# PEER expert stage of a hybrid encoder block: 40 of 256 tokens by gathered rows, 216 densely, values in column form

## The reference, cut to what matters

```
q = x @ w_q                          # 8 heads x 2 halves x 128
s1, i1 = top16(q[h,0] . keys[h,0]);  s2, i2 = top16(q[h,1] . keys[h,1])
best, ci = top16(s1 + s2)            # 16 of 256 pairs per head
idx = e1*128 + e2;  g = softmax(best)    # 128 experts per token
act = gelu(x . u_tab[idx])
out = sum over the 128 picks of g * act * v_tab[idx]
```

## Time and profile before

| what | us |
|---|---|
| median of 3 runs (2036.15 to 2037.81) | 2036.79 |
| span of the profiled execution, first to last instruction | 2033.2 |
| PE busy (share of the span) | 1985.5 (98%) |
| DVE busy | 1344.0 (66%) |
| ACT busy | 864.8 (43%) |
| POOL busy | 318.4 (16%) |
| moved by DMA | 356.87 MB, mean 176 GB/s |

### The profile page before, as it was taken

The page is one execution under the profiler, slowest core; times in us unless marked ns, Lnnn a source line. Parts: engine busy times, 40 slices in busy tenths (PEclk is TensorE's granted clock), DMA queues, the critical chain, the costliest instruction groups (busy, mean ns, idle before and its releaser), DMA issues.

```text
span 2033.2 us, 32153 instructions
## 1 busy us (share of the span) xinstructions
PE 1985.5 (98%) x10414; PEld 1694.7 (83%) x10414; DVE 1344.0 (66%) x2052; ACT 864.8 (43%) x1085; POOL 318.4 (16%) x228
## 2 busy tenths in 40 slices
PE   8999979899999999999999999999999999999997
PEld 6887768788878888888888888888888888888886
DVE  4447765554898963466666666777777766666665
ACT  5544644444444444433333334333333334444444
POOL 1003320000434444311111111111111110000000
PEclk9999989999999999999999999999999999999999
DMA  7665435554555555554454455555555556666664
GB/s 250 186 186 152 143 114 183 200 194 158 186 173 188 174 188 186 186 165 160 161 163 160 161 165 179 183 165 165 166 164 164 164 158 218 195 192 191 194 193 148
DMA packets 97137, 356.87 MB, mean 176 GB/s; under 512 B 10864, under 2 KB 10896, under 8 KB 96320
## 3 DMA queue, kind: packets, MB, share of 16 engines
q1 hardware_dynamic: 95472, 347.65, 54.0%
q0 software_dynamic: 1184, 6.00, 0.9%
q10 hardware_dynamic: 432, 2.62, 0.4%
HBM read 352.03 MB, written 4.19 MB: 175 GB/s over the span
## 4 chain that ended last, share of the span: by engine, by line
PE 89%; DVE 6%; ACT 1%; DMA 1%; issue 1%; DVEq 0%; ACTq 0%; SPq 0%
PE PS L1071 24%; PE PS L1049 16%; PE PS L1054 15%; PE PS L1081 12%; PE PS L1058 8%; PE PS L1052 8%; PE PS L1231 5%; DVE LO L598 2%; DMA RAW<-wq_t 1%; PE PS L1024 1%; ACT HI L309 0%; PE PS L1260 0%; DVE store L799 0%; DVE CI L817 0%; DVE CAND L830 0%
## 5 line engine op out<-in xcount | busy, mean ns | idle before, releaser
L309 ACT ACTIVATE HI<-RAW 128x1024 fp32r<-128x1024 f32 x656 | 696.2, 1062 | 1035.2 <-DMA RAW<-peer_v 356.2
L598 DVE TENSOR_TENSOR LO<-RAW,HI 128x1024 fp32r<-128x1024 f32 x576 | 710.3, 1233 | 591.0 <-PE PS L1054 343.6
L1071 PE MATMUL PS<-xT,HI 128*128 128x512 f32 x2304 | 596.0, 396 | 2.0 <-DVE xT L625 1.2
L1071 PEld LDWEIGHTS PS<-xT,HI 128*128 128x128 f32 x2304 | 414.6, 189 | 74.7 <-issue 1.4
L1081 PEld LDWEIGHTS PS<-xT,LO 128*128 128x128 f32 x2304 | 313.7, 190 | 30.3 <-DVE LO L598 7.4
L1081 PE MATMUL PS<-xT,LO 128*128 128x256 f32 x2304 | 321.1, 282 | 6.1 <-DVE LO L598 6.1
L1049 PE MATMUL PS<-HI,WHL 128*128 128x512 f32 x1020 | 320.2, 395 | 1.3 <-DVE WHL L933 1.3
L1054 PE MATMUL PS<-HI,WHL 128*128 128x512 f32 x1020 | 314.7, 390 | 0.0
L1054 PEld LDWEIGHTS PS<-HI,WHL 128*128 128x128 f32 x1020 | 191.4, 188 | 40.4
L298 POOL TENSOR_TENSOR ONE<-ONE,EG 128x256 f32<-128x256 f32 x128 | 113.2, 884 | 706.6 <-DVE ONE L899 706.6
L1049 PEld LDWEIGHTS PS<-HI,WHL 128*128 128x128 f32 x1020 | 186.8, 188 | 36.6 <-DVE store L799 1.6
(11 more groups left out here) (168 smaller groups left out, 1249.5 us busy)
## 6 DMA issues: line engine op xcount, KB each, us to landing
RAW<-u_t SPq DMA_DIRECT2D x256, 512.0 KB, 3.7
RAW<-peer_v SPq DMA_DIRECT2D x256, 512.0 KB, 5.0
RAW<-w_in SPq DMA_DIRECT2D x80, 512.0 KB, 3.7
RAW<-w_out SPq DMA_DIRECT2D x32, 512.0 KB, 3.8
RAW<-wq_t SPq DMA_DIRECT2D x32, 512.0 KB, 4.7
x_spill<-X POOLq DMA_DIRECT2D x2, 1024.0 KB, 11.7
ACC<-x_spill ACTq DMA_DIRECT2D x2, 1024.0 KB, 9.4
out<-ACC SPq DMA_DIRECT2D x4, 512.0 KB, 3.7
```

The source lines that it names most:

```text
L309: nc.scalar.activation(HI[:, slot, :], RAW[:, slot, :], ACT.Copy).then_inc(hi_ready, 1)
L598: v.tensor_tensor(LO[:, u % 2, :], RAW[:, u % 4, :], HI[:, u % 4, :].bitcast(FP32), ALU.subtract).then_inc(lo_ready[u % 2], 1)
L1071: return mm(PS[:, bank, :], HI[:, u % 4, cols], xT[:, k].rearrange("p a t -> p (a t)"), start=k == 0, stop=k == KT - 1)
```

## The change

216 tokens (ND) stay dense. The last 40 (NS) are computed by gathered rows. For these, three picks of each token lie on 3 x 40 = 120 partitions (SROWS), so that the 128 picks need 43 steps (NG): POOL gathers 120 rows of u_tab (8 KB each) by an indirect DMA into PICKED; DVE multiplies by the token rows X4 and sums (`dot`); after 43 of these one gelu and one gate multiply; then 43 gathers of rows of v_tab, each added to ACC4 by DVE with its factor. There is one PICKED buffer, so each gather waits for the DVE instruction before it. Dots stand at 24 score steps three key indices apart (49 to 118), at 121, 123, 125, 127, and at value units 2 to 58, every fourth; additions at units 64 to 232, every fourth.

Score units: 8 matmuls of 432 and 8 of 216 columns; the low parts of unit n-1 are interleaved with the high parts of unit n. Value units take the column form too: the v_tab tile is stationary, WHL streams (432 and 216 columns), all 128 key indices accumulate in 8 PSUM banks for one half of the width, then for the other; no flushes by group, but a turn between the halves and a transposition at the end. The ring has 6 slots, LO overwrites RAW. One spread of 3 tokens covers all key indices: 72 in all, from key index 48 on. For key indices past 48 + b the gates are copied into `store` by ACT (`put_gates`) and the gelu result is multiplied in later (`land`). The tile with the 40 tokens is chosen first (TILE_ORDER). POOL also moves the token rows for X4 and reads the picks back through DRAM. The low parts that POOL makes: the odd units from 5 on in the score stage, every fourth in the value stage.

```diff
-TOKB = 4
-N_BATCH = T // TOKB
-E2A = NKEYS // 2
+NS, ND = 40, 216
+SLOTS, NG = 3, 43
+SROWS = SLOTS * NS
+TILE_ORDER = (1, 0)
+CHOICE0 = 2
+TOKB = 3
+N_BATCH = ND // TOKB
+SPREAD0 = 48
+SPREAD_END = SPREAD0 + N_BATCH
+DOT_STEPS = list(range(SPREAD0 + 1, SPREAD_END - 1, 3)) + list(range(SPREAD_END + 1, NKEYS, 2))
+DOT_UNITS = [2 + 4 * i for i in range(NG - len(DOT_STEPS))]
+ACC0 = DOT_UNITS[-1] + 6
+ACC_UNITS = [ACC0 + 4 * i for i in range(NG)]
+def by_pool(n):
+    return n % 2 == 1 and 5 <= n < N_U or n >= N_U and n % 4 == 3
...
+            def low(n):
+                pool.wait_ge(top_ready, n + 1)
+                nc.gpsimd.tensor_tensor(RING_LO[:, n % RING, :], RING_RAW[:, n % RING, :],
+                                        HI[:, n % HI_SLOTS, :].bitcast(FP32), ALU.subtract).then_inc(low_pool, 1)
+            def gather(table, g):
+                pool.indirect_dma_start(PICKED[0:SROWS, :], None, table,
+                                        bass.IndirectOffsetOnAxis(PK4[0:SROWS, 0, g:g + 1], 0)).then_inc(row_ready, 16)
...
+            for v in range(N_V):
+                if by_pool(N_U + v):
+                    low(N_U + v)
+                if v - 1 in DOT_UNITS:
+                    g = len(DOT_STEPS) + DOT_UNITS.index(v - 1) + 1
+                    pool.wait_ge(dots, g)
+                    if g < NG:
+                        gather(peer_u, g)
+                    else:
+                        gather(peer_v, 0)
+                if v - 1 in ACC_UNITS[:-1]:
+                    g = ACC_UNITS.index(v - 1) + 1
+                    pool.wait_ge(accs, g)
+                    gather(peer_v, g)
...
+            def top(n):
+                act.wait_ge(ring_ready[n % RING], 16 * (n // RING + 1))
...
+                    act.wait_ge(top_used, n - HI_SLOTS + 1)
+                    act.wait_ge(low_pool if by_pool(n - HI_SLOTS) else low_dve, LOW_COUNT[n - HI_SLOTS])
+                nc.scalar.activation(HI[:, n % HI_SLOTS, :], RING_RAW[:, n % RING, :], ACT.Copy).then_inc(top_ready, 1)
...
+            def dot(g):
+                dve.wait_ge(row_ready, 16 * (g + 1))
+                v.tensor_tensor_reduce(PICKED[0:SROWS, :], PICKED[0:SROWS, :], X4[0:SROWS, :], 1.0, 0.0, ALU.mult, ALU.add,
+                                       DOTS[0:SROWS, g:g + 1]).then_inc(dots, 1)
...
+            for j in range(NKEYS):
+                low(2 * j + 2)
+                low(2 * j + 3)
+                sum_halves(j)
+                if j >= CHOICE0:
+                    piece()
+                    piece()
+                b = j - SPREAD0
...
+                if 0 < b <= N_BATCH:
+                    apply_gates(b - 1)
+                if 0 <= b < N_BATCH:
+                    one_hots(b)
+                if b > 0:
+                    land(j - 1)
+                if j in DOT_STEPS:
...
+                    dot(DOT_STEPS.index(j))
+            land(NKEYS - 1)
...
+            for u in range(N_V):
+                low(N_U + u + 2)
+                if u + 2 < N_V:
+                    weight_lo(u + 2)
+                if u == NKEYS - 1:
+                    for i in range(DT):
+                        flush(0, i, OUTA)
+                if u in DOT_UNITS:
+                    dot(len(DOT_STEPS) + DOT_UNITS.index(u))
...
+                if u in ACC_UNITS:
+                    g = ACC_UNITS.index(u)
+                    dve.wait_ge(row_ready, 16 * (NG + g + 1))
+                    if g:
+                        dve.wait_ge(accs, g)
+                        ins = v.scalar_tensor_tensor(ACC4[0:SROWS, :], PICKED[0:SROWS, :], DOTS[0:SROWS, g:g + 1],
+                                                     ACC4[0:SROWS, :], ALU.mult, ALU.add)
...
+            for n in range(N_U):
+                j = n // 2
+                pe.wait_ge(top_ready, n + 1)
...
+                if n:
+                    low_wait(n - 1)
+                for kk in range(DT):
+                    ins = score_high(n, kk)
...
+                    if n:
+                        ins = score_low(n - 1, kk)
...
+                if n % 2 == 0 and 0 <= j - 2 - SPREAD0 < N_BATCH:
+                    spread(j - 2 - SPREAD0)
```

More of the change, by code:

```diff
@@ L305, in _ @@
+            pool.wait_ge(x1_back, 16 * TT)
+            pool.wait_ge(accs, NG)
+            for s in range(SLOTS):
+                if s:
+                    pool.wait_ge(sparse_added, 16 * s)
+                pool.dma_start(X1R[S0:P, TT - 1, :], ACC4[s * NS:(s + 1) * NS, :], accum_op=ALU.add)\
+                    .then_inc(sparse_added, 16)
         @block.scalar
@@ new lines, in _ @@
+            for n in range(4):
+                top(n)
+            for j in range(NKEYS):
+                top(2 * j + 4)
+                top(2 * j + 5)
+                if j in (2, 4):
+                    first_scores_out(j // 2 - 1)
+                if j in GATES_AT:
+                    gates_exp(GATES_AT.index(j))
+                if j in PICKS_AT:
+                    picks_to_rows(PICKS_AT.index(j))
+                if 0 <= j - 1 - SPREAD0 < N_BATCH:
+                    put_gates(j - 1 - SPREAD0)
+                gelu(j)
@@ new lines, in weight_hi @@
+            def weight_hi(v):
+                j = v % NKEYS
+                if v >= W_SLOTS:
+                    act.wait_ge(low_used, N_U + v - W_SLOTS + 1)
+                if v < NKEYS:
+                    act.wait_ge(g_mul, N_BATCH)
+                    if j >= SPREAD0:
+                        act.wait_ge(landed, j - SPREAD0 + 1)
+                nc.scalar.activation(WHL[:, v % W_SLOTS, 0, :], store[:, j, :], ACT.Copy).then_inc(w_hi, 1)
+            for v in range(3):
+                weight_hi(v)
@@ new lines, in _, with final_squares @@
+            for v in range(N_V):
+                if N_U + v + 4 < N_U + N_V:
+                    top(N_U + v + 4)
+                if v + 3 < N_V:
+                    weight_hi(v + 3)
+                if v == DOT_UNITS[-1] + 2:
+                    act.wait_ge(dots, NG)
+                    nc.scalar.activation(DOTS[0:SROWS, :], DOTS[0:SROWS, :], ACT.Gelu_apprx_tanh).then_inc(dots_gelu, 1)
+            nc.scalar.activation(GM[:, 2, 0:1], GM[:, 1, 0:1], ACT.Sqrt).then_inc(warm, 1)
+            def final_squares(tt, half):
+                act.wait_ge(out_added, (2, 4, 6, 8)[2 * half + tt])
+                if tt:
+                    act.wait_ge(sparse_added, 16 * SLOTS)
+                squares(X1R[:, tt, half * HALF:(half + 1) * HALF], 2 * half + tt, FJ[:])
@@ L980, in _, with piece @@
-            values(0, first=True)
-            values(1, second=True)
-            with dve.Fori(2, SPREAD2 - 1) as g:
-                values(g)
-            values(SPREAD2 - 1, next_late=True)
-            values(SPREAD2, spread=False, late=True)
-            with dve.Fori(SPREAD2 + 1, N_VG - 1) as g:
-                values(g, spread=False)
-            values(N_VG - 1, spread=False, next_late=True)
+            def piece():
+                o = 0 if done[0] < PIECES else 1
+                if done[o] < PIECES:
+                    next(pieces[o])
+                    done[o] += 1
@@ L1301, in _, with low_wait, score_high @@
-            values(0, first=True)
-            with pe.Fori(1, SPREAD2) as g:
-                values(g)
-            pe.wait_ge(g_read, 2 * N_BATCH)
-            with pe.Fori(SPREAD2, N_VG - 1) as g:
-                values(g, spreads=False)
-            values(N_VG - 1, spreads=False, last=True)
+            def low_wait(n):
+                pe.wait_ge(low_pool if by_pool(n) else low_dve, LOW_COUNT[n])
+            def score_high(n, kk):
+                j, half = divmod(n, 2)
+                k = DT * half + kk
+                return mm(PS[:, j % S_BANKS, 0:2 * ND].rearrange("p (a t) -> p a t", a=2),
+                          HI[:, n % HI_SLOTS, kk * P:(kk + 1) * P], xT[:, k, :, 0:ND], start=k == 0, stop=False)
```

660 lines of the change are left out of this document (339 added, 321 removed).

## The result

The change takes 2200.3 us (median of 4 runs, 2187.3 to 2209.7) where the kernel before takes 2037.3: a ratio of 1.079, 95% interval 1.074 to 1.084. It is 163 us slower, forecast was 87 us faster. The profiled execution took 2192.5 us, with a span of 2190.7.

The account below looks back on a forecast made before the run. PE, busy 98% of the span, was taken as the bound. Start 475.4, score stage 776, value stage 674 and end 21.6 gave 1947 us of span, plus 3.6 around it 1951, say 1950, against 2036.8; range 1850 to 2055.

Parts of the forecast that it names:

- ACT 1.4 us per unit. These fit.: Value stage: ACT's 1.4 us per unit and DVE's 7.5 of 9.45 us per four units fit beside PE's work.
- the landing of 8.0 us: Value stage: a gather lands 8.0 us after issue, 7.1 for size plus 0.9 for indices and ring; cycle 10.5 us.
- the dots of the score stage: Score stage: 24 dots beside spreads stall PE, 23 us at least, 80 with POOL's low part in front; 45 taken.
- ACT waiting on RING loads: A sign that would show the prediction wrong: ACT waits for the ring's loads; no size given.
- The matmul steps: Both stages: high steps 196.7 (scores) or 193.4 ns (values), lows 102.1; 1217 us for 256 units of each, against 1411.
- rival 1: Both stages: all hidden, gathers land within 7 us, DVE and POOL seldom collide; 1833 us, half way 1870; chance 0.25 together.
- rival 3: Value stage: the gather chain becomes the bound, each us of landing costs 58 us; 2096 us at 10.5; chance 0.18.
- The gathers may not [fit].: Value stage: with one PICKED buffer, gather, dot and semaphores form a cycle; to fit 9.45 us, gathers must land in 7.0.
- Against: 424 GB/s with large transfers.: Value stage: argument against rival 3, whose loads and gathers want 313 to 326 GB/s in all.
- rival 2: Value stage: v_tab's rows 1 MB apart limit loads to 187 GB/s, 2.80 us per unit; 1994 us in all; chance 0.10.
- The choice's stall of 55 us: Score stage: PE waits for DVE's low parts behind the choice's 41 pairs of pieces; 24 to 77 us, 55 taken.
- The clock: Score and value stages: PE's granted clock was 1.00 (2.4 GHz) before, and matmul steps were priced at 2.4 GHz.

Follow-up runs that it names:

- e6_dense_swap: Changed kernel without the gathered tokens' path and with ScalarE rounding weights of unit v+3 before ring unit v+4 in the value stage: 1866.4 us, ratio 0.917.

## Why the prediction was wrong

Two terms failed, both in the value stage, which was put at 674 us and took 873: the sentence "ACT 1.4 us per unit. These fit.", which gave the order of work no cost, and the landing of 8.0 us, with nothing for what gathers do to the ring loads. A third term, the dots of the score stage, was mis-sized (45 us, measured 80). One of the prediction's own signs of being wrong, ACT waiting on RING loads, stands at 475 us.

**Right or nearly.** The matmul steps: 205 and 103 ns against 196.7 or 193.4 and 102.1, a unit of 2.45 against 2.39 and 2.36. Over 512 units that is 1254 us instead of 1217, a term 37 us short: on top of the stream of a high matmul lie 25 ns, not 13 to 17. Lows show no floor at 110 or 119 ns. By the weight load of the Trainium skill, "TensorE: Matmul & The Clock Gate", section on LDWEIGHTS, the prediction had a bound of 106.7 ns for them; the trace has 103. Spreads and start were near, the end was 5 us short. Two sums of the prediction slip a little: 58 cycles of four units leave 24 units, not 26 (5 us), and 5.1 - 4.78 us per key index is 0.32, not 0.4 (3 us). The dense part at its best, 1866 us, is about what rival 1 gives half way (1870), but it has no gathers: no run came near the first rival's 1833.

**"A gather lands in 8.0 us."** It lands in 10.2 to 10.5, inside the prediction's own bounds (up to 11). Its working would then give 2096 us by rival 3, the right sign, 104 us short. The step took 7.6 x 0.94 from a 1 MB load at a quiet moment and added 0.9 for indices and ring. Plain rows in order landed in 8.8 to 9.3 us: over the 7.1 us for size, 1.7 to 2.2 us are there without scatter and indices, and these add 1.2 to 1.4. This was a range that reached to the truth and a value taken at its friendly end. And 2096 us would have been right by luck in part: in the change the cycle did not set the pace, as the plain rows and the short dots show.

**"ACT 1.4 us per unit. These fit."** This step failed outright. It is 84 us in the dense part and 41 in the full change. It adds up busy times of an engine that works in order and never asks what stands in front of what. The weights stood behind a wait for a load; e6_dense_swap shows that moving one line gives the 84 us back in the dense part. The order stands in the program of the change. POOL's low part, released by the same ACT step, can then meet VectorE's weight part, as in the chain above. The Trainium skill, page "SBUF — State Buffer", section "SBUF: two separate sides", calls it an exclusive lock between GpSimd and a VectorE instruction with two inputs in SBUF; 2.50 us for a 0.37 us instruction agrees with that, as the earlier trace rows did. The prediction used it for the score stage and forgot it in the value stage. With the order mended, taking POOL's low parts away was worth 22 us.

**"The gathers may not [fit]."** The cycle of gather and addition was the right mechanism, but in the change it was not yet the wait that counted (54 us). It came up only after the order was mended (137 us) and was then one of two waits side by side. The missing term is what gathers do to the other queue: ring loads of 5.0 us became 5.9 in the median and 12 at times, with six slots that give them four units of 2.45 us, less 1.06 for ACT. The prediction priced each transfer by itself.

**"Against: 424 GB/s with large transfers."** The engines' time ran out at 276 GB/s. The prediction had the numbers for it: 0.61 of the engines at 187 GB/s is 307 GB/s at 1.00, and it wanted 313 to 326. It held a single 5 us window against that. The best version with all gathers has 665.9 us, not the 609 of rival 1.

**Row pitch (rival 2).** Its price of 43 us is refuted: loads from rows 8 KB apart landed in 5.8 us, from rows 1 MB apart in 5.9. The rule in the Trainium skill, "DMA: Bandwidth & Descriptors", section "Latency and other measured facts", bears on pitches of 512 KiB and more; at this kernel's rate, with 4 KB pieces, the trace does not show it. With both buffers, this pattern and the gathers together moved 276 GB/s.

**The dots of the score stage.** 45 us was taken from a range of 23 to 80; the change against the dense part gives 817 - 737 = 80, the upper bound. From 800 to 1200 us PE made 2301 matmuls where the dense part made 2716, that is 61 us lost for 20 dots, 3.1 us each instead of 1.9. A VectorE that is nearly full is not the cause: without gathers it was busy 78% of this window and PE made just as few matmuls, with the swap in the dense part it was busy 88% and PE never paused (windows of the change, of the dense part, of the run without gathers, of the dense part with the swap):

```profile
800.00:1200.00 400.00, 357.43 (x2301) 341.41 (x2299) 356.66 (x523) 161.54 (x302) 184.91 (x82) 0.97 0.72 210
```
```profile
800.00:1200.00 400.00, 400.00 (x2716) 390.99 (x2715) 296.21 (x553) 190.93 (x351) 172.57 (x73) 1.00 0.60 190
```
```profile
800.00:1200.00 400.00, 359.81 (x2287) 347.47 (x2286) 313.51 (x526) 160.36 (x301) 156.49 (x61) 0.94 0.50 159
```
```profile
800.00:1200.00 400.00, 399.69 (x2712) 390.49 (x2710) 351.07 (x550) 196.06 (x347) 171.33 (x72) 1.00 0.63 190
```

So a dot of 2.28 us in front of the low parts is enough for the loss, whichever of VectorE's instructions POOL then stretches. Gathers alone, with short dots, are enough too: u_tab's loads then landed in 7.0 us in the median (3.6 in the dense part). How the two share the 80 us of the change stays open. The choice's stall of 55 us was somewhat high: the two dense runs' 737 and 727 us, less 683 of PE's work (256 units of 2.45 us, and 56 beside them) and the 8 of the later stalls, leave 46 and 36.

**The clock.** The prediction held it at 1.00. It was 0.93 in the value stage, and a longer wait is followed by a slow restart, which cost 1.9 us after the 5.73 us in the chain above. PE was busy 707 us for work of 256 x 2.45 = 627 us, so up to 80 us of the loss are steps at the lower level, a part of the stage's 199 us and not on top of them. Once the waits were gone it came back: 0.98 with both buffers, 1.00 in the dense part with the swap.

In sum, between the dense part at its best (1866) and the change (2200) lie 334 us: 84 of the dense part's order of work, 155 in the value stage for gathers that met one buffer and a short ring, 80 in the score stage for dots and gathers, the rest the end and what runs differ by. They are counted down one after the other and are no prices of single cures: in the full change the order alone gave 41 us, POOL's low parts 22, both buffers 126 and half rows 13. With the order, POOL's part and both buffers mended it is 1.3% faster than before, with half rows 1.9%.

## What to carry to other kernels

Before a second stream of transfers is added, multiply each transfer's engine time (share x window / count) by how often it comes: the larger of this sum and the compute's own time is the floor. Buffers and order bring the time down to the floor (here from 13.0 us per four units to 11.0), below it only cheaper or fewer bytes do (10.4 with half rows, 9.9 with 60 rows). Where two waits can hold the same unit, cure both before judging either; alone, each looked worthless here. And read each in-order engine's program for what stands behind a wait on a load, not only its busy share.

## What the runs showed of the hardware that was not expected

- 120 rows of 8 KB, gathered beside a ring of 512 KB loads, take 4.2 to 4.4 us of all 16 DMA engines and land 10.2 to 10.5 us after issue; their 8 KB packets take 0.564 to 0.567 us in the median (0.307 at the lowest), gathered 4 KB ones 0.25. The 1 MB load of final_gain in 7.6 us before took 11.1 in the change.
- The DMA share of 1.00 was reached at 276 GB/s with 8 KB gathers, and of 1.02 at 295 with half rows.
- After it had stood still for 5.73 us TensorE stepped at 0.39 and 0.18 us for 3.75 us before it was back at 0.21 and 0.10; after 0.87 us of standing still (at 1659.13) it did so from its second high matmul on.
- A matmul of 432 columns stepped at 205 ns and one of 216 at 103, when they alternate.
